# The last expert pair's weight loads: three double chunks as whole 32 KB rows, three halves in one piece each

## The reference

```python
u = xb @ w_up[e] + b_up[e]
glu = jnp.minimum(u[:, 0::2], SWIGLU_LIMIT)
lin = jnp.clip(u[:, 1::2], -SWIGLU_LIMIT, SWIGLU_LIMIT)
a = glu * jax.nn.sigmoid(SWIGLU_ALPHA * glu) * (lin + 1)
return a @ w_down[e] + b_down[e]
```

## Time and profile before

| | us |
|---|---|
| median of 3 executions | 1172.48 (1172.28 to 1172.68) |
| profiled execution, its own time | 1172.19 |
| its span, first to last instruction | 1170.4 |
| TensorE matmuls busy | 1109.7 (95% of the span) |
| queue q1 (SyncE's loads), mean share of 16 DMA engines | 89.0% |

### The profile page before, as it was taken

The page is one execution under the profiler, slowest core; times in us unless marked ns, Lnnn a source line. Parts: engine busy times, 40 slices in busy tenths (PEclk is TensorE's granted clock), DMA queues, the critical chain, the costliest instruction groups (busy, mean ns, idle before and its releaser), DMA issues.

```text
span 1170.4 us, 13933 instructions
## 1 busy us (share of the span) xinstructions
PE 1109.7 (95%) x5564; PEld 494.9 (42%) x5593; DVE 420.7 (36%) x853; ACT 183.0 (16%) x355; POOL 76.9 (7%) x136
## 2 busy tenths in 40 slices
PE   9999999899999999999999999999999999999998
PEld 6688888463333333333333333333333333333332
DVE  4864543663263323323232323232323232222222
ACT  2122211520041010101111110101010101010101
POOL 1654034000000000000000000000000000000000
PEclk9999999899999999999999999999999999999999
DMA  9975454849999999999999999999999999999997
GB/s 317 332 250 179 146 164 107 373 157 398 429 419 423 423 428 429 431 432 431 431 433 431 430 435 431 430 432 432 431 432 433 431 430 433 432 430 432 426 424 289
DMA packets 45119, 444.15 MB, mean 379 GB/s; under 512 B 5772, under 2 KB 11612, under 8 KB 28076
## 3 DMA queue, kind: packets, MB, share of 16 engines
q1 hardware_dynamic: 39336, 435.08, 89.0%
q0 software_dynamic: 4896, 7.93, 2.8%
q10 hardware_dynamic: 852, 0.64, 0.2%
HBM read 440.23 MB, written 2.36 MB: 378 GB/s over the span
## 4 chain that ended last, share of the span: by engine, by line
PE 59%; DMA 36%; DVE 2%; issue 1%; ACT 1%; ACTq 0%; SPq 0%
PE pA L1648 26%; PE pB L1648 26%; DMA ring<-in_w_up 18%; DMA ring<-in_w_down 12%; PE pM L1648 6%; DMA area<-in_w_up 5%; PE pM L1651 1%; PE pA L1651 1%; DMA x<-in_x_prompt 1%; ACT area L990 0%; DVE hn L1542 0%; DVE x L1500 0%; DVE area L1544 0%; DVE area L1536 0%; DVE area L1069 0%
## 5 line engine op out<-in xcount | busy, mean ns | idle before, releaser
L1648 PE MATMUL pA<-ring,hn 128*64 128x512 f32 x1536 | 352.5, 602 | 23.6 <-DMA ring<-in_w_up 23.6
L1648 PEld LDWEIGHTS pA<-ring,hn 128*64 128x64 f32 x1536 | 105.3, 137 | 219.5 <-issue 185.5
L1648 PE MATMUL pB<-ring,area 128*64 128x512 f32 (+2 forms) x784 | 174.1, 605 | 11.5 <-DMA ring<-in_w_down 5.8
L1648 PE MATMUL pB<-area,ring 128*128 128x264 f32 (+1 forms) x928 | 183.4, 388 | 0.0
L1648 PEld LDWEIGHTS pB<-area,ring 128*128 128x128 f32 (+1 forms) x928 | 144.1, 175 | 34.8 <-issue 4.0
L1648 PE MATMUL pA<-area,hn 128*64 128x512 f32 x512 | 119.3, 610 | 10.3 <-DMA area<-in_w_up 10.3
L1648 PEld LDWEIGHTS pB<-ring,area 128*64 128x64 f32 (+2 forms) x784 | 58.9, 137 | 108.6 <-issue 95.6
L1500 DVE TENSOR_TENSOR x<-pM,x 128x512 f32<-128x512 f32 x60 | 40.1, 691 | 147.3 <-PE pM L1648 147.2
L978 ACT ACTIVATE area<-area 128x512 f32<-128x512 f32 x30 | 18.9, 630 | 385.4 <-DVE area L1483 385.4
L1415 DVE COPY conv_row<-pM 128x512 f32<-128x512 f32 x30 | 20.6, 686 | 146.7 <-PE pM L1648 146.7
L1648 PEld LDWEIGHTS pA<-area,hn 128*64 128x64 f32 x512 | 36.1, 139 | 74.6 <-issue 59.7
(11 more groups left out here) (311 smaller groups left out, 839.8 us busy)
## 6 DMA issues: line engine op xcount, KB each, us to landing
ring<-in_w_up SPq DMA_DIRECT2D x36, 4096.0 KB, 29.8
ring<-in_w_down SPq DMA_DIRECT2D x18, 4096.0 KB, 29.2
area<-in_w_up SPq DMA_DIRECT2D x12, 4096.0 KB, 30.2
ring<-in_w_up SPq DMA_DIRECT2D x17, 2048.0 KB, 13.6
area<-in_w_down SPq DMA_DIRECT2D x6, 4096.0 KB, 30.0
ring<-in_w_in SPq DMA_DIRECT2D x22, 1024.0 KB, 13.1
ring<-in_w_up SPq DMA_DIRECT2D x14, 1024.0 KB, 9.3
ring<-in_w_down SPq DMA_DIRECT2D x13, 1024.0 KB, 25.9
```

What stands on the lines that cost most here:

```text
L1648: return pe.matmul(out, w, m, start=start, stop=stop, skip_group_check=True)
```

## The change

Double chunks 0, 1 and 2 of the last pair are loaded by one DMA each, as in the loop. `LAST_ROWS` loses its entries for j = 7, 8 and 9, so these halves are one DMA each. j = 10 and 11 stay cut. The waits in `loaded` follow: for b below `LAST_WHOLE` the first half waits for `unit_full`, and the second has no wait. What is computed is the same, and nothing changes in any other pair.

```diff
--- before.py
+++ after.py
@@ -226,7 +226,8 @@
 EARLY = {2: 2, 3: 2, 4: 2, 5: 4, 6: 2, 7: 2, 8: 2, 9: 2, 10: 2, 11: 2}
 
 
-LAST_ROWS = {7: (2, 2), 8: (2, 2), 9: (2, 2), 10: (2, 2), 11: (2, 1, 1)}
+LAST_ROWS = {10: (2, 2), 11: (2, 1, 1)}
+LAST_WHOLE = 3
 
 
 HN_HALVES = [(0, 0), (1, 0), (0, 1), (1, 1)]
@@ -693,6 +694,9 @@
                 turn = 2 * PAIR_CHUNKS * (PAIRS // 2 - 1) + ODD + b
                 sp.wait_ge(ring_free, LOOP_FREED + turn - UNITS_KEPT + 1)
                 u = UNIT[turn % UNITS_KEPT]
+                if b < LAST_WHOLE:
+                    whole(b, PAIRS - 1, turn)
+                    continue
                 for h in range(2):
                     j = 2 * b + h
                     if j not in LAST_ROWS:
@@ -2007,11 +2011,11 @@
                         pe.wait_ge(early_piece[early_j], 16 * (EARLY[early_j] - 1))
                     if last and j in LAST_ROWS and not whole:
                         pe.wait_ge(last_piece[j, 0], 16)
-                    elif (last or halves) and h == 0:
-                        n = 1 + len(HALF_PAIRS) * PAIR_CHUNKS // UNITS_KEPT if last else 1
-                        at_ = turn if last else PAIR_CHUNKS * (g - 1) + b
-                        pe.wait_ge(unit_half[u], 16 * (n + at_ // UNITS_KEPT))
-                    elif last or halves or h == 0:
+                    elif (halves or last and b >= LAST_WHOLE) and h == 0:
+                        n = len(HALF_PAIRS) * PAIR_CHUNKS // UNITS_KEPT + (b >= LAST_WHOLE + UNITS_KEPT) if last else \
+                            (PAIR_CHUNKS * (g - 1) + b) // UNITS_KEPT
+                        pe.wait_ge(unit_half[u], 16 * (n + 1))
+                    elif last and b >= LAST_WHOLE or halves or h == 0:
                         pe.wait_ge(unit_full[u], 16 * PAIRS2_TURNS * pairs2 + 16 * (turn // UNITS_KEPT + 1))
                     return unit(u)[:, SLOT * h:SLOT * h + SLOT]
 
```

## The result

| | before | with the change |
|---|---|---|
| median of 20 executions, us | 1171.88 (1170.94 to 1173.17) | 1173.87 (1172.73 to 1175.76) |
| ratio to before, 95% interval | | 1.0015 (1.0008 to 1.0022) |
| profiled execution, its span, us | 1172.19, 1170.4 | 1173.06, 1171.2 |

The medians are 1.99 us apart; the forecast was 1.65. The interval lies above 1, so the change is slower, and by 0.15% in place of the 0.2% that I had set as the bound, though the interval reaches 0.22%. (The 1171.88 is over 20 executions, the 1172.48 known earlier over the first three.)

The account below looks back on a forecast made before the run. Transfers bound the loop; in pair 15 the end is TensorE's work after three late waits for transfers. +3.27 - 1.62 = +1.65 us on 1172.48 gave 1174.1 us, range 1172.9 to 1175.3.

Parts of the forecast that it names:

- TensorE falls behind by 3.27 at up(6): Pair 15: waiting for whole double chunks delays up(0), up(2), up(4) by 1.92, 2.66, 3.27 us; up(6) keeps +3.27.
- 1.62 is taken up, at j = 8, j = 10 and j = 11: Pair 15 after up(6): waits of 0.67, 0.71 and 0.24 us are no longer needed, -1.62 us in sum.
- The loads are worth 0.44 and it reaches nothing: Pair 15's loads: j = 10's first piece lands at most 0.44 us earlier; costed at nothing since TensorE is later.
- The loads of b = 4 and 5 are released later without harm: Pair 15's queue: these loads are released about 1.9 and 2.7 us later, but the queue stays full; cost nothing.
- `y_first` is there with 0.3 us to spare: At j = 10, ScalarE's copies end before `first_expert_sums` needs them, margin 0.3 us; failure would add a few tenths.
- The end did not stay with the transfers: Rival, end of pair 15: TensorE takes up its whole lag, the end moves by -0.44 to 1172.0 us; chance 0.07.
- The lag was taken up: Rival, pair 15, j = 8 to 11: lag not taken up, other waits replace those removed; 1175.75 us, +0.28%; chance 0.13.
- A fixed price for each DMA: Rival, the loads: six DMAs fewer save over 0.67 us each, at most 2.4 each, giving 1159.6 us; chance 0.02.
- the last rival: TensorE's clock falls: nothing seen for it, clock 1.00 in pairs 13 and 14; no separate chance, within the tail.

Follow-up runs that it names:

- the change's second profile: The changed kernel profiled once more, no edit: one execution, 111.32 us from pair 14's up(0) to the last scatter, against 109.75 in the kernel before.
- the whole chunks alone: Kernel before with double chunks 0 to 2 of the last pair whole, j = 7, 8 and 9 still cut: ratio to before 1.0013.
- the waits alone: Kernel before, all loads unchanged, but TensorE waits for both halves ahead of up(0), up(2) and up(4) of the last pair: ratio 1.0018.
- six DMAs more: Kernel before with j = 0 to 5 of the last pair also cut in two: ratio to before 1.0001.
- uncut halves: Kernel before with j = 7, 8 and 9 of the last pair in one piece each, double chunks 0 to 2 still in halves: ratio 1.0003.
- the two with filling matmuls: Kernel before with only double chunk 0 whole, plus four or two matmuls of constants ahead of up(0)'s wait: ratios 1.0014 and 0.9994.
- the version with two filling matmuls: Kernel before with only double chunk 0 of the last pair whole and two matmuls of constants ahead of up(0)'s wait: ratio 0.9994.
- one double chunk whole: Kernel before with only double chunk 0 of the last pair loaded whole, no filling: ratios 1.0008 and, run again, 1.0007.

## Why the prediction was right, step by step

- *TensorE falls behind by 3.27 at up(6).* 3.20 without a fall of the clock, and 1.94, 0.58 and 0.54 of idle time at up(0), up(2) and up(4), near what the loop has. Shown by the change's second profile and by the whole chunks alone (3.21); that the waits make it and not the loads, by the waits alone. At up(4) the lag is the forecast one: 1130.71 - 1053.01 = 77.70 less 1127.67 - 1053.23 = 74.44 is 3.26. The last 0.06 go between up(4) and up(6), which takes 8.35 with the change and took 8.41 before. That is a fourth place at which TensorE met a transfer, and the prediction had it at nothing ("None of up(0), up(2), up(4) and up(6) has a wait in front of it"); six DMAs more make it visible.
- *1.62 is taken up, at j = 8, j = 10 and j = 11.* 3.20 - 1.57 = 1.63. In all nine profiles in which TensorE is more than 1.6 us late at up(6), from 1.86 to 4.60 us, the lag at up(6) less the delay of the end is 1.62 or 1.63, with a fall of the clock or without. This is the best supported term of the sum.
- *The loads are worth 0.44 and it reaches nothing.* About 0.5, and nothing.
- *The loads of b = 4 and 5 are released later without harm.* j = 10 was issued at 1129.57 - 1051.54 = 78.03 in place of 74.31, 3.7 later where I had 2.7, and landed earlier all the same. The fall of the clock is in the 3.7; in the second profile, without it, it is 1129.97 - 1053.01 = 76.96, 2.65 later.
- *`y_first` is there with 0.3 us to spare.* ScalarE's copies with the change:

```profile
1154.40 0.59 ACT L997 ACTIVATE area<-pB 64x512 f32<-64x512 f32 x1 [3.86 <-PE pB L1652]
1155.01 0.59 ACT L998 ACTIVATE area<-pB 64x512 f32<-64x512 f32 x1
```

They end at 1155.60, and `first_expert_sums` follows the run of 24 from 1150.70, at 1150.77 + 5.30 = 1156.07 by the chain. The margin was 0.4 to 0.5, and no wait stands there.
- *The rivals.* The end did not stay with the transfers (they came about 0.5 earlier and the end 2.02 later). The lag was taken up. A fixed price for each DMA is ruled out by the six DMAs more: 0.08 us each and not 0.67. The upper bound that I gave for it, 2.4 us from 21.75 / 9, was a misreading: 8.4 of the 21.75 are a wait on `ring_free`, so the nine issues took 1.75 + 11.58 = 13.3 us, or 1.5 each, and 1159.6 should have been about 1165. The page of the Trainium skill named in the prediction, "DMA: Bandwidth & Descriptors" (section "Anatomy of one DMA — SWDGE (gpsimd) path"), has 2.0 us for a DMA by itself, and no run here bears on that case.
- **The step that was wrong** is the last rival, where I wrote of the clock that there was "nothing here for it". The clock did fall at up(0), in five of the seven profiles that have an idle time of 1.94 to 2.03 ahead of up(0) of pair 15, and in none of the five that don't (before, uncut halves, six DMAs more, and the two with filling matmuls). I had argued that the loop has the same gap and a clock of 1.00. That was true of the two pairs that I looked at. The same trace, further back, has it otherwise. Up(0) of pair 7 in the kernel before:

```profile
645.29 5.35 PE L1648 MATMUL pA<-ring,hn 128*64 128x512 f32 x16 [1.86 <-DMA ring<-in_w_up]
```

It takes 5.35 in the pairs 6, 7 and 8 and 5.30 in pair 9, each time behind an idle time of 1.85 or 1.86, and pair 8 begins 58.27 behind pair 7, as if nothing had been. Over pairs 6 to 14 of the twelve profiles that is so at 13 of 108 up(0)s. While the loop's waits take a fall up, in pair 15 it counts. It is 0.45 us of the change's cost when it happens.
- *What was luck.* The median difference of 1.99 lies near the 2.02 with a fall, and the forecast of 1.65 near the 1.57 without one, but the interval reaches from 0.9 to 2.6 us, so the medians can't tell the two apart; that takes the profiles. The median itself, 1173.87 against a forecast of 1174.1, is closer than the terms deserve: the three executions that the forecast started from lay 0.6 above the 20, and the difference was 0.34 too small, which partly cancel.

Why the clock falls in one execution and not in the next is open, and so is why it fell in five of seven at this place and in 13 of 108 in the loop. The profiles show only what went before: idle time of about 1.95 us at that place. In both profiles in which it was filled with work the clock stayed up. That filling is what kept it up is likely and not shown: two in seven stay up without it, so two profiles would do so by chance about one time in twelve. With the three others that have no idle time there it is five of five.

No version here is shown to beat the kernel before; the version with two filling matmuls has the lower median, 1171.34 against 1172.16, but the interval holds 1 and the end stretch is 0.24 longer. What the kernel before has left in waits for transfers is 1.6 us in pair 15, and there the end follows the transfers; whole rows would give these 0.09 us a double chunk and cost up to 1.9 of waiting.

## What to carry to other kernels

Fewer, larger transfers are worth what they save only where the end follows the transfers; where the engine would otherwise start on the first half, the price is the time that it now waits for the second (1.92 us at up(0), where halves land 4.90 apart and TensorE came 3 us behind the first). Such a lag is paid down only by waits that lie behind it, so add those up first (1.62 us here): several edits share them, and their costs don't add. In a pipeline bound by transfers, a fall of the clock behind a wait was free here (the loop's pairs kept their 58.28). In the last stage it costs what no wait behind it takes up: 1.69 us with one double chunk whole, 0.45 where two waits follow, nothing to be seen where a third does. And a look at two pairs is too few to say that the clock does not fall.

## What the runs showed of the hardware that I had not expected

- TensorE's granted clock fell to 0.51 (1.2 GHz) for a stretch of up(0) after 1.95 us without work, although TensorE had been busy for 53 of the 58 us before. From pair 6 on it happened only behind idle times of 1.85 us and more ahead of an up(0), and not behind each of them. Sixteen instructions took 5.35 us in place of 3.65.
- A DMA more in a full queue cost 0.08 us. But SyncE was held up at the issue itself: with 18 loads in pair 15 single issues took up to 4.95 us and the last five 11.58 together, with 12 loads the last five took 2.23. The late issues were not on the path here, since the transfers ahead of them were still under way.
- The instructions of the filling matmuls, whose weights are 128 columns wide, took 3.53 us for eight, 0.44 each. Those of the experts' matmuls, 64 columns wide, take 3.44 for sixteen, 0.215 each. A single one of them is no shorter (the profile has 596 ns on average against 592, with modelled ends). They come in pairs that write to different halves of the output's partitions, and the timeline has their weight loads two by two, 0.43 us apart: two at a time take as long as one of the wide ones. That is why the filling cost twice what I had worked out.
